# Attention heads moved between the chunks of the last eight input units of a hybrid decoder step

## The reference, cut to what matters

```python
h = rmsnorm(x, norm1_w[l])
z = h @ w_in[l]                       # retention q,k,v,gate | cq, ckv, kr | gx, gg
o_ret, S_ret = retention_mixer(...)   # 4 heads, chunks of 128, per-head decay
q_lat, q_rope, ckv, k_rope = mla_project(cq, ckv, kr, ...)
o_lat = attend(l, q_lat, q_rope, ckv, k_rope)   # 8 heads; softmax over keys
y_mla = einsum('bthr,rhd->bthd', o_lat, w_uv)
y_rg, rg_buf, rg_h = rglru_mixer(gx, gg, ...)   # conv, gates, scan, gelu gate
x = x + concat([y_ret, y_mla, y_rg]) @ w_out[l]
x = x + conv_ffn(rmsnorm(x, norm2_w[l]), ...)

# attend, prompt: s = q_lat.ckv + q_rope.k_rope, masked; p = softmax(s); o = p.ckv
# attend, samples: the same over past_lat = pool_lat[page_table] (16 pages of 128 rows
# per sample), past_rope = pool_rope[page_table], and the sample's own new key
```

## Time and profile before

| | |
|---|---|
| median of 3 runs | 1519.16 us (1518.94 to 1522.99) |
| the profiled execution | 1520.06 us |
| its span, first to last instruction | 1518.0 us |
| mean granted TensorE clock | 0.959 of full speed |
| TensorE matmuls busy | 1398.6 us (92%) |
| VectorE busy | 785.3 us (52%) |
| ScalarE busy | 521.6 us (34%) |
| chain that ended last | PE 82%, SP's queue 6%, issue 4%, DVE 4%, ACT 3%, DMA 1% |

### The profile page before, as it was taken

The page is one execution under the profiler, slowest core; times in us unless marked ns, Lnnn a source line. Parts: engine busy times, 40 slices in busy tenths (PEclk is TensorE's granted clock), DMA queues, the critical chain, the costliest instruction groups (busy, mean ns, idle before and its releaser), DMA issues.

```text
span 1518.0 us, 28455 instructions
## 1 busy us (share of the span) xinstructions
PE 1398.6 (92%) x11664; PEld 1294.0 (85%) x11664; DVE 785.3 (52%) x1331; ACT 521.6 (34%) x795; POOL 22.4 (1%) x43
## 2 busy tenths in 40 slices
PE   7998887789999999999999889776999999999997
PEld 7987555469999999999998875554899999999996
DVE  5545344325666535666534553443366664366654
ACT  5232244314433323334432413433153332233332
POOL 1000000000000000000100000000000000000000
PEclk9999889989999999999999997899899999999998
DMA  9336211342232233222471552024322222323222
GB/s 344 106 108 164 80 28 34 108 138 84 84 98 91 77 98 111 85 74 90 146 235 57 146 152 68 1 65 115 115 85 96 86 88 87 104 97 98 66 88 74
DMA packets 86707, 154.55 MB, mean 102 GB/s; under 512 B 12913, under 2 KB 45842, under 8 KB 86450
## 3 DMA queue, kind: packets, MB, share of 16 engines
q1 hardware_dynamic: 84002, 142.90, 30.5%
q0 software_dynamic: 2576, 9.84, 1.7%
HBM read 146.31 MB, written 6.58 MB: 101 GB/s over the span
## 4 chain that ended last, share of the span: by engine, by line
PE 82%; SPq 6%; issue 4%; DVE 4%; ACT 3%; DMA 1%; DVEq 0%; ACTq 0%
PE PS L1227 65%; SPq L338 4%; PE PS L1538 2%; PE PS L1631 2%; PE PS L1236 1%; PE PS L1243 1%; PE PS L1252 1%; ACT PR L659 1%; ACT WH L438 1%; PE PS L1316 1%; PE PS L1520 1%; SPq L332 1%; PE PS L1485 1%; PE PS L1530 1%; PE PS L1467 1%
## 5 line engine op out<-in xcount | busy, mean ns | idle before, releaser
L1227 PE MATMUL PS<-XNH,WH 128*128 128x260 f32 x2176 | 449.0, 288 | 14.9 <-DVE WL L748 9.2
L1227 PE MATMUL PS<-XNH,WL 128*128 128x260 f32 x2176 | 442.6, 285 | 0.0
L1227 PE MATMUL PS<-XNL,WH 128*128 128x260 f32 x2176 | 442.2, 285 | 0.0
L748 DVE TENSOR_TENSOR WL<-RAW,WH 128x1024 fp32r<-128x1024 f32 x200 | 244.8, 1224 | 252.8 <-ACT WH L438 252.8
L438 ACT ACTIVATE WH<-RAW 128x1024 fp32r<-128x1024 f32 x200 | 211.8, 1059 | 475.4 <-PE PS L1227 474.5
L1227 PEld LDWEIGHTS PS<-XNH,WH 128*128 128x128 f32 x2176 | 338.9, 190 | 20.6 <-issue 14.6
L1227 PEld LDWEIGHTS PS<-XNH,WL 128*128 128x128 f32 x2176 | 338.4, 190 | 0.5
L1227 PEld LDWEIGHTS PS<-XNL,WH 128*128 128x128 f32 x2176 | 337.6, 189 | 0.5
L1227 PE MATMUL PS<-HL,WH 128*128 128x260 f32 x704 | 142.0, 283 | 0.0
L1227 PE MATMUL PS<-HH,WL 128*128 128x260 f32 x704 | 141.5, 282 | 0.0
L1227 PE MATMUL PS<-HH,WH 128*128 128x260 f32 x704 | 141.2, 282 | 0.0
(11 more groups left out here) (241 smaller groups left out, 1293.1 us busy)
## 6 DMA issues: line engine op xcount, KB each, us to landing
RAW<-in_units SPq DMA_DIRECT2D x136, 512.0 KB, 3.5
KT<-in_kat SPq DMA_DIRECT2D x256, 80.0 KB, 2.2
KA<-in_ka SPq DMA_DIRECT2D x256, 64.0 KB, 1.8
RAW<-in_units SPq DMA_DIRECT2D x32, 384.0 KB, 3.1
RAW<-in_units SPq DMA_DIRECT2D x32, 320.0 KB, 2.8
X<-in_x SPq DMA_DIRECT2D x16, 260.0 KB, 4.3
C<-in_const POOLq DMA_DIRECT2D x1, 2196.0 KB, 10.6
out_y<-X SPq DMA_DIRECT2D x8, 260.0 KB, 7.1
```

Source lines behind the costliest of these rows:

```text
L748: V_.tensor_tensor(WL[:, u % NHL, :], RAW[:, u % NRAW, :], WH[:, u % NHL, :].bitcast(F32), ALU.subtract)\
L1227: i = mm(ps(name)[0:rows, hb, 0:HB], w, x[:, x0_ + k, hb * HB:(hb + 1) * HB], start=(first and k == k0 and s == 0), stop=(last and k == k1 ...
```

## The change

It moves the attention of the prompt and much of the sample attention into the input projection, and rewrites how one head is computed.

- **Order.** Head h (0 to 7) has its scores in unit 8 + h, its turning and its value product in the next unit (head 7 behind unit 15). All eight page scores stand in units 8 to 12, the sample softmax in units 12 to 15. Rotary queries and values are computed in units 6 and 7. Behind unit 15 stand: turning and values of head 7, the retention products, `dp0` to `dp7` among them, `dz`, `dy`. ACT's, DVE's and SP's orders are rewritten to suit; the gates of unit 8 go to unit 10.
- **Scores.** Queries and keys of a pair are copied by one ACT instruction (`QK`, 128 by 1024) instead of four; no 96-row operands are built. The scores of a head are summed from the mask (128 rows), the main part (the 64 rows of the head) and the rotary part (32 rows, `QR` with `Z[.., Z_KR]`), each its own matmul, for each of four query blocks.
- **Division.** DVE no longer scales the exponentials (four instructions); it makes four diagonal matrices `DIAG` of 1/sum (one instruction) and PE turns and divides in one matmul of plain floats in place of the transpose.
- **Results** of the heads go to `AO`, and in four larger pieces to `XNH` and `XNL`.
- **Raw weights.** Units 4 to 15 use only two of the four `RAW` places, since `AO` lies in the other two.
- **Pages** are asked for by SP whole samples at a time, at new places of its order; the places in memory are the same two.
- PSUM has a fifth chain of turns: `PS3` is divided into its two banks.

```diff
+IN_SLOT = [0, 1, 3] + [(_u + 1) % 2 for _u in range(3, N_IN_U)]
+SIDE_TILES = {
+    1: [("n1", 2)], 3: [("nckv", 2)], 5: [("ncq", 3), ("pkr", 2)],
+    6: [("q8", 3), ("qr0", 2), ("g0r", 3), ("g0i", 2)],
+    7: [("pq8", 3), ("pqr0", 2), ("qr1", 3), ("ql", 2), ("pqr1", 3), ("v01", 2), ("v23", 3)],
+    8: [("qk0", 0), ("ds0", 3), ("s0", 2), ("ds1", 3)],
+    9: [("pz0", 1), ("qk1", 1), ("ds2", 3)],
+    10: [("ds3", 3), ("g1r", 0), ("g1i", 0), ("ds4", 3)],
+    11: [("ds5", 3), ("pz1", 1), ("qk2", 1), ("ds6", 3)],
+    12: [("ds7", 3), ("pz2", 0), ("dn", 3)],
+    13: [("dm", 3), ("pz3", 1), ("qk3", 1), ("db", 3)],
+    14: [("rt0", 0), ("dd", 3)],
+    15: [("dt0", 3), ("rt1", 1), ("dt1", 3), ("dk", 1)],
+}
...
+PROGRAM += [("t7", 2), ("tb7", 4), ("dq", 3), ("kv", 0), ("o7", 3), ("rs0", 1), ("rs1", 0), ("dp0", 3), ("dp1", 4), ("du", 2),
+            ("ro", 1), ("dp2", 3), ("do", 0), ("dp3", 4), ("gm0", 2), ("gm1", 1), ("dp4", 3), ("dp5", 4), ("gv0", 0), ("gv1", 2),
+            ("dp6", 3), ("dp7", 4), ("dz", 3), ("dy", 3)]
...
+        def score_at(q, a, b):
+            i, k, o = ((2, 1, 384), (3, 0, 0), (2, 1, 0), (2, 0, 0))[q]
+            return PS[i][:, k, o + a:o + b]
...
+                one(l, 4)
+                pages(l, 0, 0)
+                one(l, 5)
+                pages(l, 0, 1)
+                for u in range(6, 12):
+                    one(l, u)
+                sp.wait_ge(*filled(l, "ds0"))
+                pages(l, 0, 2)
+                sp.wait_ge(*filled(l, "ds1"))
+                pages(l, 0, 3)
+                one(l, 12)
+                sp.wait_ge(*filled(l, "ds2"))
+                pages(l, 0, 4)
+                one(l, 13)
+                sp.wait_ge(*filled(l, "ds3"))
+                pages(l, 0, 5)
+                sp.wait_ge(*filled(l, "ds4"))
+                pages(l, 0, 6)
+                one(l, 14)
+                sp.wait_ge(*filled(l, "ds5"))
+                pages(l, 0, 7)
+                sp.wait_ge(*filled(l, "ds6"))
+                pages(l, 1, 0)
+                one(l, 15)
+                sp.wait_ge(*filled(l, "ds7"))
+                pages(l, 1, 1)
+                one(l, 16)
+                one(l, 17)
+                for b in range(2, NB):
+                    sp.wait_ge(*filled(l, f"dp{b - 2}"))
+                    pages(l, 1, b)
+                    if b == 5:
+                        sp.wait_ge(*at("ao_lo", l, 4))
+                        one(l, 18)
+                        one(l, 19)
+                sp.wait_ge(*filled(l, "ro"))
+                sp.wait_ge(*filled(l, "dp4"))
                 sp.wait_ge(*at("pret_saved", l, 16))
-                sp.wait_ge(*filled(l, "dp4"))
                 for k in range(KD):
-                    sp.dma_start(X[:, k, :], y_o[k] if l else xd[k]).then_inc(x_back, 16)
-                sp.wait_ge(*filled(l, "dy"))
+                    if k == KD - 1:
+                        sp.wait_ge(*filled(l, "dy"))
+                    sp.dma_start(X[:, k, :], y_o[k] if l else xd[k]).then_inc(x_in[k], 16)
...
+                def exponential(h):
+                    act.wait_ge(*at("nmax_ready", l, h + 1))
+                    act.wait_ge(*at("gx_saved", l, 32))
+                    for q in range(4):
+                        o = 128 * (q * (q + 1) // 2)
+                        i = act.activation(PR[:, o:o + 128 * (q + 1)], score_at(q, 0, 128 * (q + 1)), ACT.Exp,
+                                           scale=SCALE, bias=STAT[:, q:q + 1], accum_out=STAT[:, 8 + q:9 + q])
+                    i.then_inc(emptied(f"s{h}"), 1)
...
+                queries_and_keys(0)
+                gelu_and_root(0)
+                score_copy(0)
+                exponential(0)
+                score_copy(1)
                 after_unit(8)
+                turned(0)
+                attended(0)
+                queries_and_keys(1)
+                exponential(1)
+                score_copy(2)
                 after_unit(9)
+                score_copy(3)
+                turned(1)
+                gate(1, 0)
+                attended(1)
+                gate(1, 1)
+                exponential(2)
+                score_copy(4)
+                decay(1)
                 after_unit(10)
+                score_copy(5)
+                turned(2)
+                attended(2)
+                queries_and_keys(2)
+                exponential(3)
+                score_copy(6)
+                gelu_and_root(1)
                 after_unit(11)
+                score_copy(7)
+                turned(3)
+                attended(3)
+                exponential(4)
                 after_unit(12)
...
+                def shares(h):
+                    dve.wait_ge(*freed(l, f"s{h}"))
+                    link(V_.reciprocal(STAT[:, 12:16], STAT[:, 8:12]))
+                    eye = const("ident").rearrange("p (a n) -> p a n", a=1).broadcast_to([P, 4, P])
+                    inv = STAT[:, 12:16].rearrange("p (q a) -> p q a", a=1).broadcast_to([P, 4, P])
+                    V_.tensor_tensor(DIAG[:, :, :], eye, inv, ALU.mult).then_inc(S["p_ready"][0], 1)
...
+                def scores(h):
+                    name, c, rope_rows = f"s{h}", h // 4, slice(32 * HEAD_AT[h % 4], 32 * HEAD_AT[h % 4] + 32)
+                    tile(l, name)
+                    if h:
+                        pe.wait_ge(*freed(l, f"tb{h - 1}"))
+                    pe.wait_ge(*freed(l, f"qk{h // 2}"))
+                    pe.wait_ge(*at("kr_copied", l, 3))
+                    pe.wait_ge(*at("roped", l, c + 1))
+                    for q in (3, 2, 1, 0):
+                        mine = slice(P * q, P * q + P)
+                        mm(score_at(q, P * q, P * q + P), idt, const("causal"), start=True, stop=False)
+                        if q:
+                            mm(score_at(q, 0, P * q), QK[half(h), 0, mine], QK[half(h), 1, 0:P * q], start=False, stop=False)
+                        mm(score_at(q, P * q, P * q + P), QK[half(h), 0, mine], QK[half(h), 1, mine], start=False, stop=False)
+                        last = mm(score_at(q, 0, P * q + P), QR[rope_rows, c, mine], Z[rope_rows, Z_KR, 0:P * q + P],
+                                  start=False, stop=True)
+                    last.then_inc(full(name), 1)
+
+                def turned(h):
+                    pe.wait_ge(*at("p_ready", l, h + 1))
+                    tile(l, f"t{h}")
+                    tile(l, f"tb{h}")
+                    for kt in (0, 1, 3, 2):
+                        for q in range(kt, 4):
+                            o = P * (q * (q + 1) // 2) + P * kt
+                            last = mm(turned_at(kt, P * (q - kt), P * (q - kt) + P), PR[:, o:o + P], DIAG[:, q, :], start=True, stop=True)
+                        if kt == 3:
+                            last.then_inc(full(f"t{h}"), 1)
+                    last.then_inc(full(f"tb{h}"), 1)
...
+                unit(9, 0, 2)
+                turned(0)
+                unit(9, 2, 3)
                 swap_pair(0)
+                unit(9, 3, 4)
+                scores(1)
+                unit(9, 4, 5)
+                attended(0)
+                unit(9, 5, 6)
+                queries_and_keys(1)
+                unit(9, 6, 7)
+                page_scores(2)
+                unit(9, 7)
+
+                unit(10, 0, 1)
+                page_scores(3)
+                unit(10, 1, 2)
+                turned(1)
+                unit(10, 2, 3)
+                gate(1, 0)
+                unit(10, 3, 4)
+                scores(2)
+                unit(10, 4, 5)
+                attended(1)
+                unit(10, 5, 6)
+                gate(1, 1)
+                unit(10, 6, 7)
+                page_scores(4)
+                unit(10, 7)
+
...
+                turned(7)
+                pe.wait_ge(*at("newp_diag", l, 2))
+                tile(l, "dq")
+                mm(single("dq", slice(0, NB), slice(0, 256)), const("ones", cols=(0, NB)), SMALL[:, 176:432], start=True, stop=True)\
+                    .then_inc(full("dq"), 1)
...
+                attended(7)
+                chunk_scores(0)
+                chunk_scores(1)
+                values_attended(0)
+                values_attended(1)
+                pe.wait_ge(*at("vm_ready", l, 4))
...
```

More of the change, by code:

```diff
@@ L60 @@
 UW = KD * P
[L64 to L81, removed]
+HEAD_AT = (0, 2, 1, 3)
@@ new lines, in _ @@
+                unit(6, 0, 2)
+                pe.wait_ge(small_in, l * 80 + 80)
+                pe.wait_ge(*freed(l, "ncq"))
+                tile(l, "q8")
+                for c in range(6):
+                    for k in range(2):
+                        last = mm(ps("q8")[:, 0, NB * c:NB * c + NB], UQ[:, k, P * c:P * c + P], Z[:, 1 + k, SEQ:T],
+                                  start=(k == 0), stop=(k == 1))
+                last.then_inc(full("q8"), 1)
+                rope_queries(0)
+                unit(6, 2, 5)
@@ new lines, in _ @@
+                for h in range(MH):
```

(50 more changed lines are left out.)

960 lines of the change are left out of this document (460 added, 500 removed).

## The result

The changed kernel takes 1608.25 us (median, 1604.13 to 1611.23), the kernel before beside it 1521.08: a ratio of 1.0567, 95% interval 1.0531 to 1.0604. The forecast had the sign and not the size: 1547 us, range 1511 to 1573. The profiled execution spans 1607.4 us against 1518.0 before, 89.4 us more: 50.3 of them are there when layer 0's output projection begins (372.93 against 322.64), 39.1 come in layer 1.

The account below looks back on a forecast made before the run. TensorE, busy for 92% of the span, was taken as the bound, SP's page requests in the tail. Per layer 154.5 + 11.5 + 8.7 + 8 + 76 = 258.7 us against 245.1; 27 us in two layers gave 1547, range 1511 to 1573.

Parts of the forecast that it names:

- work, units 8 to 15: TensorE's products in units 8 to 15 of one layer, counted at full clock: 154.5 us, with 17.5 us of added score work.
- 96 changes of rows: New scores in units 8 to 15: 12 row-count changes a head, 96 a layer, at 0.12 us each: 11.5 us.
- waits: TensorE waiting between a head's scores and its turning: head 0 3.3, head 5 1.9, head 7 0.5, small ones 1.3: 7.0 us.
- clock: One fall of TensorE's clock in units 8 to 15, as after the longer gaps before the change: 1.7 us.
- ahead of unit 8: Rotary queries, their swaps and values moved ahead of unit 8, less a covered wait in unit 7: 8 us net.
- behind unit 15: From unit 15's end to the output projection: 11 us to dp0's end, then SP's requests for six samples, landing and rest: 76 us.
- the flaw named in it: Tail before the output projection: heads leave the time SP asks for value pages, and that time stays, 74 us before, 76 after.
- three signs of being wrong: Forecast wrong if the tail is under 70 us, a row change is free, or units 8 to 15 take over 190 us.
- About the same: Rival: row changes in the scores cost nothing, waits as computed; 2.1 us more a layer, 1523 us; chance 0.20.
- Faster: Rival: units 8 to 15 run at full clock without a wait; 6.6 us less a layer, 1506 us; chance 0.17.
- Much slower: Rival: each of eight turnings waits some 2 us more and the clock falls with it; 1577 us; chance 0.13.
- the last rival: Page requests: all are SP's already, so that part of the change alone moves nothing; no chance given.

## Why the prediction was right and wrong

By its own terms, layer 0 (us). The work at full clock is from the kernel with 128 rows: 155.44 us from unit 8 to the end of unit 15, less 3.1 of waits and 1.5 of clock.

| term | forecast | measured |
|---|---|---|
| work, units 8 to 15 | 154.5 | 150.8 |
| 96 changes of rows | 11.5 (0.12 each, 0 to 14.1) | 18.5 (0.19 each) |
| waits | 7.0 | 0.8 |
| clock | 1.7 | 34 |
| ahead of unit 8 | 8 | 10.0 |
| behind unit 15 | 76 | 78.5 |
| sum | 258.7 | 292.6, against 293.9 in the trace |

- **The direction and the flaw named in it were right**: "the heads leave the time in which SP asks for the value pages, and that time stays". Before, 74.0 us of the stretch held five heads; after, 78.5 us hold only the turning and the values of the last. The term was 2.5 us short: dp0 ended 9.6 us behind unit 15 and not 11, the requests took 1.1 more than counted, and the rest lies in small gaps between the parts.
- **The work** was right to 2.5%.
- **The step that failed is the clock.** The forecast read the clock only as an answer to gaps (45.5 us idle, 0.91) and so gave the new order, which has no gaps, a clock near 1 (one fall, 1.7 us). The clock fell instead with every head's scores, with 0.76 us of waits in all units together, and the split of the scores brought that about (the new order without it has 0.98). In the earlier trace rows the nearest case, 128 and 64 rows in turn, ran on at full clock (1.00 from 160 to 168 us), and so it did in the kernel with 8 changes of this kind. No row of the kernel before showed 32-row parts beside 64-row ones over many columns, and no bound was set for a price of that kind. The term is some 32 us short (34 against 1.7), of the 35.2 us by which layer 0 is over the forecast. Of the forecast's three signs of being wrong this one came: units 8 to 15 over 190 us.
- **A change of rows** was mis-sized: 0.12 was taken, with the earlier trace rows giving 0.08 to 0.14, and it measured 0.19. Both bounds came from mean times of a few pipelined matmuls; why they were low is not shown. It adds 7.0 us. The rule of the Trainium skill (TensorEngine Tiling, Key Properties) that a change of mode drains the engine was the one that spoke against the change, and the 0.19 us a change agree with it.
- **The waits** did not come, in part because the half clock stretched the work that stood ahead of the turnings: 6.7 us lie between the end of head 0's scores (105.37) and its turning (112.05). In the kernel with 128 rows throughout, head 0 does wait, 1.61 us where 3.3 were forecast, and all waits of its units are 3.1 us, so the term was too large at full clock as well:

```profile
103.84 2.50 PE L1528 MATMUL PS<-DIAG,PR 128*128 128x128 f32 x20 [1.61 <-DVE DIAG L1034]
```

- **The rivals.** "About the same" (1523) was to hold if changes of rows cost nothing: the kernel with 128 rows throughout is that case, with the same columns, and took 1523.87. So the sum was right for everything but the changes and the clock, in part by luck: the work was counted 3.7 us too high and the waits too high, the parts ahead and behind too low. "Faster" (1506), without waits too, was not reached; with the split's columns taken out as well it ran at 1496.8. "Much slower" had a fall of the clock behind waits: the fall came, without the waits. Nothing in the runs speaks against the last rival, that the move of the page requests by itself gains nothing.

## What to carry to other kernels

Count TensorE's row counts before splitting a product: a change between 128, 64 and 32 rows costs 0.19 us here, and one between 128 and 96 nothing. Pad with zero rows rather than split, as long as the columns are the same. And check an order without gaps for its clock too: full occupation with narrow matmuls ran at half clock for some 69 of 205 us. When a tail is set by a queue's requests, spread the requests over two queues before moving the work that used to cover it: that alone brought the kernel before to 1510.37, and with the whole new order it is 1509.39.

## What the runs showed of the hardware that was not expected

- The granted clock fell with TensorE busy for 204.58 of 205.34 us, in matmuls of few rows, and stayed full in kernels with more waits (0.99 with 3.4 us of 157.9).
- 12 changes and 32-row parts cost 84 us against the same columns over 128 rows; either one thinned out (8 changes without 32 rows, or 8 with 128-row neighbours) cost 22 and 20 us.
- From 128 to 96 rows nothing is paid.
- GpSimd issues page requests almost as fast as SP: 0.56 us each and 0.43 for reading four numbers, 0.67 a page, against SP's 0.62 with its reading.
